# Taking the first RMSNorm's factor out of the activations and putting it on the results

## What is computed

```python
h = rmsnorm(x, norm1[l])                 # x * rsqrt(mean(x*x) + EPS) * norm1
z = h @ w_in[l]
(z_rx, z_ry, z_q, z_kc, z_vc, z_ks, z_vs, z_kw, z_vw, z_ng, z_mg) = split(z)
xr = rg_lru(causal_conv(z_rx, conv_w[l], conv_b[l]), ...)
y_a = (xr * jax.nn.gelu(z_ry)) @ w_rg_out[l]
q = rmsnorm(z_q, q_norm[l])
kc = rmsnorm(compress(z_kc, cmp_pos_k[l], ...), k_norm[l, 0]);  vc = compress(z_vc, cmp_pos_v[l], ...)
k_s = rmsnorm(z_ks, k_norm[l, 1]);  k_w = rmsnorm(z_kw, k_norm[l, 2])
ng = jax.nn.sigmoid(z_ng);  mg = jax.nn.sigmoid(z_mg)
y_b = nsa(q, kc, vc, k_s, z_vs, k_w, z_vw, ng) @ w_nsa_out[l]
x = x + (mg[0] * y_a + mg[1] * y_b) @ w_o[l]
x = x + (jax.nn.silu(h2 @ w_gate[l]) * (h2 @ w_up[l])) @ w_down[l]     # h2 = rmsnorm(x, norm2)
```

## Time and profile before

| | us |
|---|---|
| median of three runs | 483.1 |
| profiled execution, its own time | 483.16 |
| its span (first to last instruction) | 481.4 |
| TensorE busy in the span | 475.2 |
| VectorE busy | 354.7 |
| ScalarE busy | 280.3 |
| GpSimd busy | 16.3 |

### The profile page before, as it was taken

The page is one execution under the profiler, slowest core; times in us unless marked ns, Lnnn a source line. Parts: engine busy times, 40 slices in busy tenths (PEclk is TensorE's granted clock), DMA queues, the critical chain, the costliest instruction groups (busy, mean ns, idle before and its releaser), DMA issues.

```text
span 481.4 us, 7336 instructions
## 1 busy us (share of the span) xinstructions
PE 475.2 (99%) x2795; PEld 410.0 (85%) x2795; DVE 354.7 (74%) x630; ACT 280.3 (58%) x451; POOL 16.3 (3%) x27
## 2 busy tenths in 40 slices
PE   7999999999999999999999999999999999999997
PEld 7998998788999777877788888888888888888886
DVE  3999899699897886766754758777777777764332
ACT  4755886775777897566753435755555555453320
POOL 2000210220000000000000000000000000000000
PEclk9999999999999999999999999999999999999999
DMA  8755979724243346243434452655555455555402
GB/s 309 264 170 195 372 290 257 274 88 175 88 144 120 135 159 231 91 174 95 167 116 147 150 205 83 247 197 199 208 199 176 176 181 191 207 208 175 174 1 87
DMA packets 12993, 85.78 MB, mean 178 GB/s; under 512 B 1568, under 2 KB 1824, under 8 KB 3104
## 3 DMA queue, kind: packets, MB, share of 16 engines
q1 hardware_dynamic: 12096, 82.32, 47.5%
q0 software_dynamic: 432, 2.10, 1.5%
q10 hardware_dynamic: 432, 0.91, 0.5%
HBM read 83.22 MB, written 1.05 MB: 175 GB/s over the span
## 4 chain that ended last, share of the span: by engine, by line
PE 98%; DVE 0%; POOL 0%; issue 0%; ACT 0%; POOLq 0%; DVEq 0%
PE bank L1121 19%; PE bank L1122 19%; PE bank L1123 19%; PE bank L1159 16%; PE bank L1162 8%; PE bank L1295 3%; PE bank L1242 2%; PE bank L1331 2%; PE bank L1535 1%; PE bank L1304 1%; PE bank L1252 1%; PE bank L1379 1%; PE bank L1314 1%; PE bank L1338 1%; PE bank L1335 1%; PE bank L1279 0%
## 5 line engine op out<-in xcount | busy, mean ns | idle before, releaser
L680 DVE TENSOR_TENSOR w_lo<-raw,w_hi 128x2048 fp32r<-128x2048 f32 x71 | 162.5, 2290 | 49.9 <-ACT w_hi L375 49.6
L375 ACT ACTIVATE w_hi<-raw 128x2048 fp32r<-128x2048 f32 x72 | 138.0, 1917 | 48.0 <-PE bank L1123 41.4
L1159 PE MATMUL bank<-h_hl,w_hi 128*128 128x512 f32 x336 | 80.3, 391 | 0.0
L1159 PEld LDWEIGHTS bank<-h_hl,w_hi 128*128 128x128 f32 x336 | 61.7, 188 | 11.9
L1121 PE MATMUL bank<-w_hi,h_hl 128*128 128x512 f32 x160 | 63.6, 398 | 0.0
L1123 PE MATMUL bank<-w_hi,h_hl 128*128 128x512 f32 x160 | 62.5, 390 | 0.0
L1122 PE MATMUL bank<-w_lo,h_hl 128*128 128x512 f32 x160 | 62.4, 390 | 0.0
L1121 PE MATMUL bank<-w_hi,act 128*128 128x512 f32 x150 | 59.1, 394 | 0.0
L1123 PE MATMUL bank<-w_hi,act 128*128 128x512 f32 x150 | 58.5, 390 | 0.0
L1122 PE MATMUL bank<-w_lo,act 128*128 128x512 f32 x150 | 58.4, 390 | 0.0
L1162 PEld LDWEIGHTS bank<-h_hl,w_lo 128*128 128x128 f32 x336 | 43.1, 191 | 1.6
(11 more groups left out here) (245 smaller groups left out, 740.2 us busy)
## 6 DMA issues: line engine op xcount, KB each, us to landing
raw<-stream_dram SPq DMA_DIRECT2D x72, 1024.0 KB, 4.8
w<-stream_dram SPq DMA_DIRECT2D x4, 1024.0 KB, 9.2
raw<-stream_dram SPq DMA_DIRECT2D x2, 512.0 KB, 7.5
act<-act POOLq DMA_DIRECT2D x2, 512.0 KB, 13.0
xs<-x_dram POOLq DMA_DIRECT2D x1, 1024.0 KB, 5.2
out_dram<-xs SPq DMA_DIRECT2D x3, 256.0 KB, 2.0
xs<-x_dram ACTq DMA_DIRECT2D x1, 512.0 KB, 5.0
xs<-x_dram SPq DMA_DIRECT2D x1, 512.0 KB, 4.8
```

The lines of the kernel that those rows point to most:

```text
L375: sc.activation(w_hi[:, i % HL, :], raw[:, i % RAW, :], ACT.Copy).then_inc(hi_ready, 1)
L680: ve.tensor_tensor(w_lo[:, i % HL, :], raw[:, i % RAW, :], f(w_hi[:, i % HL, :]), ALU.subtract).then_inc(lo_ready, 1)
L1159: ins = pe.matmul(acc(u + mt)[:, :], w_hi[:, s, c:c + P], a_hl[:, k, :, :].rearrange("p x s -> p (x s)"), start=n == 0, stop=n == 2 * KC - ...
```

## The change

1. TensorE transposes `x` itself, as soon as it has landed and 28 turns of the identity are done; `xn` and its two products on DVE are gone.
2. The factor goes to the results. Where tokens lie on partitions, it is a scale of an ACT instruction that was there already (keys, queries, values, the gates). Where tokens lie along the free axis (rx, kc, vc, ry), DVE makes two diagonal matrices of the factor, TensorE multiplies them by a matrix of ones (two products into bank 3), and ACT copies the result to `tok_x`, 128 x 256.
3. rx, kc and vc are copied by ACT from PSUM to SBUF (`rx_tok`, `kv_tok`; six new copies of 128 x 512), and POOL multiplies each in place by `tok_x`. ACT's tap 0, DVE's taps and DVE's position adds read these copies. ry was copied already and gets a multiply by POOL too (four of them). Semaphores `rx_scaled`, `kv_scaled`, `ry_scaled` carry this on.
4. The first half of slot 0 is split in two quarters (512 columns each), which stand between the chunks of `h` on ACT and DVE. The load of `x`'s second half is issued after that of the parameters on ACT's queue.

```diff
@@ gpsimd
             pool.memset(half[:, :], -0.5).then_inc(pool_chain, 1)
-            pool.wait_ge(pool_chain, 4)
+            pool.memset(ones_x, 1.0).then_inc(pool_chain, 1)
+            pool.wait_ge(pool_chain, 5)
...
             rsqrt(NORM_X)
+            def by_token(buf, u, scale):
+                pool.wait_ge(acc_free[u % 4], u // 4 + 1)
+                both = buf.rearrange("p (m s) -> p m s", m=2)
+                return pool.tensor_tensor(both, both, scale.unsqueeze(1).broadcast_to([P, 2, S]), ALU.mult)
+
+            pool.wait_ge(tok_x_ready, 1)
+            for r in range(4):
+                by_token(rx_tok[:, r, :], USE["rx"] + r, tok_x).then_inc(rx_scaled, 1)
             for t in range(T2):
                 rsqrt(NORM_K, t, 8)
...
+            for j, name in enumerate(("kc", "vc")):
+                by_token(kv_tok[j], USE[name], tok_x).then_inc(kv_scaled, 1)
@@ scalar
+            sc.dma_start(prm[:, :], params[:, :]).then_inc(prm_in, 16)
             sc.dma_start(xs[:, 1, :], x[P:2 * P, :]).then_inc(x1_in, 16)
-            sc.dma_start(prm[:, :], params[:, :]).then_inc(prm_in, 16)
...
-            sc.wait_ge(first_half, 16)
-            sc.activation(w_hi[:, 0, 0:1024], raw[:, 0, 0:1024], ACT.Copy).then_inc(hi_half, 1)
-            sc.wait_ge(landed[0], 16)
-            sc.activation(w_hi[:, 0, 1024:2048], raw[:, 0, 1024:2048], ACT.Copy).then_inc(hi_ready, 1)
...
+            def first_quarter(e):
+                sc.wait_ge(first_half, 16)
+                sc.activation(w_hi[:, 0, e * 512:(e + 1) * 512], raw[:, 0, e * 512:(e + 1) * 512], ACT.Copy).then_inc(hi_half, 1)
+
             sc.wait_ge(prm_in, 16)
-            chunks_hi(MISC["xT"], 0, G1)
+            chunks_hi(MISC["xT"], 0, G1, 0, 2)
+            first_quarter(0)
+            chunks_hi(MISC["xT"], 0, G1, 2, 3)
+            first_quarter(1)
+            chunks_hi(MISC["xT"], 0, G1, 3, 6)
+            sc.wait_ge(landed[0], 16)
+            sc.activation(w_hi[:, 0, 1024:2048], raw[:, 0, 1024:2048], ACT.Copy).then_inc(hi_ready, 1)
+            chunks_hi(MISC["xT"], 0, G1, 6, KC)
             split_hi(1)
+            sc.wait_ge(x_spread, 1)
+            sc.activation(tok_x, psum[3][:, 0:S], ACT.Copy).then_inc(tok_x_ready, 1)
...
+                r = i - FIRST["rx"] - 1
+                if 0 <= r < 4:
+                    u = USE["rx"] + r
+                    acc_ready(FIRST["rx"] + r)
...
+                    sc.activation(rx_tok[:, r, :], acc(u)[:, :], ACT.Copy).then_inc(acc_free[u % 4], 1)
@@ vector
-            for t in range(T2):
-                ve.tensor_scalar(xn[:, t, :], xs[:, t, :], rs[:, NORM_X, t:t + 1], None, ALU.mult).then_inc(xn_ready, 1)
-            ve.wait_ge(hi_half, 1)
-            ve.tensor_tensor(w_lo[:, 0, 0:1024], raw[:, 0, 0:1024], f(w_hi[:, 0, 0:1024]), ALU.subtract).then_inc(lo_half, 1)
...
-            chunks_lo(MISC["xT"], 0, G1, 0, 4)
+            chunks_lo(MISC["xT"], 0, G1, 0, 2)
+            ve.wait_ge(consts, 4)
+            ve.wait_ge(rs_ready, rs_count(NORM_X))
+            for t in range(T2):
+                ve.tensor_scalar(diag_x[:, t, :], ident[:, :], rsx[:, t:t + 1], None, ALU.mult).then_inc(diag_x_ready, 1)
+            first_quarter(0)
+            chunks_lo(MISC["xT"], 0, G1, 2, 3)
+            first_quarter(1)
+            chunks_lo(MISC["xT"], 0, G1, 3, 6)
...
-                        ve.wait_ge(slot_done, FIRST[name] + 1)
+                        ve.wait_ge(kv_scaled, j + 1)
@@ tensor
-            pe.wait_ge(rs_ready, rs_count(NORM_X))
-            keep_busy(6)
             for t in range(T2):
-                pe.wait_ge(xn_ready, t + 1)
+                pe.wait_ge((x_in, x1_in)[t], 16)
...
-            keep_busy(6)
+            keep_busy(4)
+            pe.wait_ge(diag_x_ready, 2)
+            for t in range(T2):
+                ins = pe.matmul(psum[3][:, t * P:(t + 1) * P], ones_x, diag_x[:, t, :], start=True, stop=True)
+            ins.then_inc(x_spread, 1)
+            keep_busy(2, 2)
...
                 pe.wait_ge(lo_half, 1)
                 for k in range(KC):
+                    if k == KC // 4:
+                        pe.wait_ge(lo_half, 2)
                     if k == KC // 2:
                         slot_ready(0)
```

More of the change, by code:

```diff
@@ L264, in hybrid_layer @@
         RS_BEFORE = [0, 1, 3, 5, 7, 8]
+        rsx = rs[:, NORM_X, :]
+        rsx_half = ss[:, NORM_X, 2:4]
         def rs_count(n, t=0):
@@ L355, in _ @@
             rsqrt(NORM_KC)
+            pool.wait_ge(tok_x_ready, 1)
+            pool.wait_ge(asq_used, 3)
+            pool.tensor_copy(tok_y, tok_x).then_inc(tok_moved, 1)
+            pool.wait_ge(tok_moved, 1)
+            for r in range(4):
+                u = USE_RY[r]
+                pool.wait_ge(acc_free[u % 4], u // 4 + 1)
+                pool.tensor_tensor(B[:, 2 * r:2 * r + 2, :], B[:, 2 * r:2 * r + 2, :], tok_y.unsqueeze(1).broadcast_to([P, 2, S]),
+                                   ALU.mult).then_inc(ry_scaled, 1)
             pool.wait_ge(y_lo_ready, 4)
@@ L434, in _ @@
                     split_hi(i + AHEAD)
+                r = i - FIRST["rx"] - 1
+                if 0 <= r < 4:
+                    u = USE["rx"] + r
+                    acc_ready(FIRST["rx"] + r)
+                    if r == 0:
+                        sc.wait_ge(ms_ready, 1)
+                    sc.activation(rx_tok[:, r, :], acc(u)[:, :], ACT.Copy).then_inc(acc_free[u % 4], 1)
+                for j, name in enumerate(("kc", "vc")):
+                    if i == FIRST[name] + 1:
+                        u = USE[name]
+                        acc_ready(FIRST[name])
+                        sc.activation(kv_tok[j], acc(u)[:, :], ACT.Copy).then_inc(acc_free[u % 4], 1)
                 r = i - FIRST["ry"] - 1
@@ L446, in _ @@
                         u = USE["vv"] + t
-                        sc.activation(v_sb[:, t, :], acc(u)[:, :], ACT.Copy).then_inc(acc_free[u % 4], 1)
+                        sc.activation(v_sb[:, t, :], acc(u)[:, :], ACT.Copy, scale=rsx[:, t:t + 1]).then_inc(acc_free[u % 4], 1)
                     sc.wait_ge(kcT_done, 1)
@@ L514, in _ @@
                     sc.wait_ge(misc_done, misc_count(m))
-                    sc.activation(gates[:, :, :, :].rearrange("p t b h -> p (t b h)"), misc(m)[:, 0:96], ACT.Tanh,
-                                  scale=0.5).then_inc(misc_free[m % 4], 1)
+                    sc.wait_ge(rs_half, 1)
+                    for t in range(T2):
+                        ins = sc.activation(gates[:, t, :, :].rearrange("p b h -> p (b h)"), misc(m)[:, 48 * t:48 * t + 48], ACT.Tanh,
+                                            scale=rsx_half[:, t:t + 1])
+                    ins.then_inc(misc_free[m % 4], 1)
                 if i == 0:
@@ L628, in _ @@
                             dst = mtt[:, t, :] if pnl < 2 else mt1[:, t, (pnl - 2) * 512:(pnl - 1) * 512]
-                            sc.activation(dst, acc(u)[:, :], ACT.Tanh, scale=0.5).then_inc(acc_free[u % 4], 1)
+                            sc.activation(dst, acc(u)[:, :], ACT.Tanh, scale=rsx_half[:, t:t + 1]).then_inc(acc_free[u % 4], 1)
                 for v in range(2):
@@ L1262, in _ @@
                     for c in (j, j + 4):
-                        ins = pe.transpose(misc(m)[:, c // 4 * S + t * P:c // 4 * S + (t + 1) * P], xn[:, t, c * P:(c + 1) * P], ident[:, :])
+                        ins = pe.transpose(misc(m)[:, c // 4 * S + t * P:c // 4 * S + (t + 1) * P], xs[:, t, c * P:(c + 1) * P], ident[:, :])
                     if t == 1:
                         ins.then_inc(misc_done, 1)
-            keep_busy(6)
+            keep_busy(4)
+            pe.wait_ge(diag_x_ready, 2)
+            for t in range(T2):
+                ins = pe.matmul(psum[3][:, t * P:(t + 1) * P], ones_x, diag_x[:, t, :], start=True, stop=True)
+            ins.then_inc(x_spread, 1)
+            keep_busy(2, 2)
             def first_x(u):
```

54 lines of the change are left out of this document (32 added, 22 removed).

## The result

The changed kernel takes 494.97 us (median of 4 runs, 493.95 to 495.86), the kernel before 483.11 (4 runs, 482.95 to 483.19): ratio 1.0243, 95% interval 1.023 to 1.0256. It is 11.9 us slower. The prediction said 483.6, with 487.2 as its upper end.

What follows compares the result with a forecast made beforehand. TensorE's own chain was taken to bound the kernel. Profiled 483.16 us plus 0.45 (0.1 at the first product, 0.35 at chunk 4), with the multiplies hidden, gave 483.6 us; the 8-in-10 range was 482.4 to 487.2.

Steps and rivals of the forecast that it cites:

- What bounds the kernel: Whole kernel: TensorE busy 475.2 of 481.4 us; only a moved first product or a wait inside the stream changes the time.
- The start: Before slot 1: first product at 12.3 instead of 12.17, slot 1 at 18.45 instead of 17.99; +0.45 us in sum.
- the gap at chunk 4: TensorE in slot 0: chunk 4 waits 0.35 us for the second half of slot 0, ready at 15.5.
- the 2.3 us allowed: Start: loading the parameters first delays x's second half by less than the 2.3 us left before the transposes.
- By this row contention costs nothing: DVE beside POOL: an instruction with two SBUF inputs took 1.23 us beside a power, 1.22 without, so multiplies add nothing.
- the likeliest case: Whole kernel: start as worked out, multiplies hidden, 483.6 us, own range 482.8 to 484.1; chance 0.50.
- POOL holds DVE up: slower: Before W1: six multiplies each cost DVE 0.62 us against about 0.95 us of slack, W1 waits 2.8, 486.4 us; chance 0.37.
- another place than W1 waits: Sign of being wrong: TensorE waits elsewhere than at W1, such as at the key transposes, which need DVE; no size given.
- I take nothing: DVE's taps and adds reading SBUF instead of PSUM: at most 1.4 us could come back; none was counted.
- A scale on an ACT instruction costs nothing: ACT instructions given the norm's factor as a scale: no added time, since chunks already have one.
- The multiply's price: POOL's multiply of 128 x 512: 0.6 to 1.2 us, hidden up to about 3 us.
- The rival of the power's price: POOL's multiplies at some 80 us each: six put hundreds of us on the chain; chance 0.02.

Runs made afterwards that it cites:

- experiment 1: Changed kernel with POOL's six multiplies of rx, kc and vc replaced by setting one column of a spare tile; ACT's copies stay: 485.72 us.
- 5: Changed kernel with each of POOL's six multiplies of rx, kc and vc turned into a copy of the tile onto itself: 489.19 us.
- 6: Changed kernel with each of POOL's six multiplies done as two of 128 x 256, the whole computation: 494.37 us.
- experiment 8: Changed kernel with TensorE turning the identity in its two long waits, 22 turns before the second gate product and 36 before W1: 492.95 us.
- experiment 3: Changed kernel without the six multiplies of rx, kc and vc and without ACT's copies of kc and vc; DVE's position adds read PSUM: 484.86 us.
- experiment 9: As experiment 3, with POOL's four multiplies of ry also turned into memsets of one column: 484.16 us.
- experiment 4: Changed kernel with a write-only POOL memset of 128 x 1280 in place of each multiply of rx, kc and vc: 490.24 us.
- experiment 7: Changed kernel with DVE multiplying rx, kc and vc as it takes them from PSUM; ACT's six copies and POOL's six multiplies gone: 491.68 us.
- experiment 2: Changed kernel without the multiplies of kc and vc; the four of rx stay: 490.63 us.

## Why the prediction was wrong

**What bounds the kernel: right.** TensorE's chain, and a wait inside the stream the only way to lose more than tenths.

**The start: right, +0.5 where +0.45 stood.** First product 12.29 (12.3), the gap at chunk 4 0.27 us (15.52 less 15.25; 0.35), slot 1 at 18.50 (18.45). One step was off without harm: x's second half landed at 8.6, so it was late by more than the 2.3 us allowed, and the transposes had begun at 8.33 with the first half. Other runs of the same start put the first product between 12.04 and 12.84 and slot 1 between 18.23 and 19.04, so that this term is 0.2 to 1.05, not a fixed half.

**The failed step: "By this row contention costs nothing, and the sum stays at +0.45."** The earlier trace rows have POOL's power beside a DVE instruction. I wrote myself that a power reads little, and still let it carry the likeliest case. A multiply is what it is not, and experiments 1, 5 and 6 show that DVE is held until a POOL instruction that streams through SBUF is through: 1.03 us beside a 1.30 us multiply, 0.35 beside a 0.61 us copy, twice 0.5 for two halves. The rule of the Trainium skill (SBUF — State Buffer, section SBUF: two separate sides) that I cited against the change was the right one for the multiplies, with the stretched rows at 23.77 and 80.35 beside it; beside the powers of the earlier trace rows it is still not borne out.

**The rival "POOL holds DVE up: slower": the mechanism, with the sizes wrong.** It priced a multiply at 0.62 us of DVE and 6 of them at 486.4; measured are about 1.03 each for five and 1.84 for one, 7.0 together. Its own sum at that price, 7.0 - 0.95, would give 489.7. What was missing for 495.0:

- The slower position adds, 2.7 us of DVE ahead of W1, used the slack up: without any multiply W1 already waited 1.3 us (experiment 1).
- No term for the clock. W1, at 0.50 behind its wait, takes 1.5 us more; experiment 8 gives 2.0 us back in all.
- Slack was counted at W1 alone. The copies of the keys have only some 0.7 us, and four multiplies are ahead of them, so TensorE waited twice, 2.56 and 4.08 us. The prediction named such a place as what would prove it wrong ("another place than W1 waits"). But by the rows it costs little here, the 0.6 us that DVE idles at 65.18, since DVE's lateness at W1 covers the rest.
- ry's multiplies cost some 0.7 us (3 against 9). I had asked only about those ahead of W1.

**Reads of SBUF: "I take nothing" was wrong in sign.** The position add takes 0.575 to 0.6 us from SBUF and 0.42 from PSUM. My estimate came from a row with unit steps; the add reads its source by a step of 16 elements. Whether it is the step or the second input in SBUF I did not try. The taps are at 0.48 us from either.

**"A scale on an ACT instruction costs nothing": not quite.** ACT's squares of the keys take 0.677 us with the scale from `rs` (L455) and took 0.589 without (L413), and the copies 0.69 for 0.60. ACT does four of these ahead of its next split, and DVE's idle time behind it is 1.87 us in the changed kernel and its variants, against 1.38 before. No run tests it by itself.

**The multiply's price: 1.30 us, above my 0.6 to 1.2.** The line through two affine selects gave half. The rival of the power's price did not come true. ACT's four copies of rx cost nothing on the chain, as said: experiment 9 has them, and loses nothing behind the start. The two of kc and vc lie in the 0.9 us of experiment 3.

From the differences of medians, run by run: start 1.05 (as it lay in 9), ry 0.7, reads from SBUF 0.9, multiplies 9.25; together 11.9. These are steps along one chain of runs, so they give the result by construction; what they show is the share of each.

## What to carry to other kernels

Before work goes to an idle GpSimd, ask what it reads. If it streams SBUF tiles beside a nearly full VectorE, most of its duration is VectorE's loss (1.03 of 1.30 us here), in whole or in pieces, and the same multiply on VectorE itself was cheaper here (0.69 us against 1.03). A row that shows two engines side by side bears on your case only if the operation has the same traffic; if it hasn't, the case is open and must not be the likeliest. And look for every place where an engine's lateness reaches the bound one: the smallest slack is met first, the wait that ends last sets the time, and a long wait costs again behind it, in clock.

## What the runs showed that I had not expected

- A write-only GpSimd instruction still holds some VectorE instructions: a TENSOR_SCALAR with one SBUF input went from 0.17 to 0.92 us beside a memset, a TENSOR_TENSOR with two stayed at 0.17 (experiment 4).
- A strided add of 64 x 256 with its source in SBUF takes 0.59 us, in PSUM 0.42.
- TensorE's clock was at 0.50 behind waits of 2.6 and 4.1 us, and at 1.00 where they were filled with turns of the identity. Behind the 1.9 us wait of experiment 7 it stayed at 1.00.
- Beside two DMA issues and the multiply behind them, a one-input DVE instruction took 2.19 us and not 0.35; beside the DMA issues alone it kept 0.35 (experiment 2).
- A start that is 0.5 us shorter in the profile did not show in the median of 11 runs, whose spread (482.47 to 483.89) was wider than that of the kernel before (482.88 to 483.49).
